# Values of recurrence and attention made as tokens by features in seven of eight mixing heads

## What is computed

```python
u = rms_norm(h, ln_mix_pre[l])
hq, hf, hi, hg, aq, ak, av = jnp.split(u @ w_in[l], split_at, axis=-1)
o_rec = hgrn2_mixer(hq, hf, hi, hg, lb_all[l], hgrn_norm[l])
o_att = dilated_attention_mixer(aq, ak, av)
mixed = jnp.concatenate([o_rec, o_att], axis=-1) @ w_out[l]
```

## Time and profile before

| | |
|---|---|
| median of 3 runs | 1771.32 us (1771.08 to 1771.66) |
| profiled execution, its own time | 1771.09 us |
| its span, first to last instruction | 1769.3 us |
| TensorE matmul busy | 1755.0 us, 99% of the span |
| DVE, ACT, POOL busy | 1254.6, 942.8 and 612.6 us |
| mean granted clock of TensorE | 0.998 |

### The profile page before, as it was taken

One profiled execution on the slowest core, in us unless ns is written; L12 is line 12 of the kernel. 1 busy time (PEld: TensorE's weight loads), 2 busy tenths in 40 slices (PEclk: granted clock), 3 DMA queues, 4 the chain that ended last, 5 costly groups with the idle time before them and its releaser, 6 DMA issues.

```text
span 1769.3 us, 29586 instructions
## 1 busy us (share of the span) xinstructions
PE 1755.0 (99%) x10201; PEld 1543.0 (87%) x10201; DVE 1254.6 (71%) x1594; ACT 942.8 (53%) x1254; POOL 612.6 (35%) x621
## 2 busy tenths in 40 slices
PE   9999999999999999999999999999999999999997
PEld 7888888888888888888888888888888888888886
DVE  6877777765598777777777644444987788887754
ACT  5544554554476555555555533334655567775532
POOL 1743345556603333111111322221262255550032
PEclk9999999999999999999999999999999999999999
DMA  8444444436565555555555555556455444444453
GB/s 314 176 177 167 165 167 167 167 143 247 184 237 189 189 190 190 190 190 190 190 190 190 169 190 186 194 185 220 168 190 202 167 167 167 167 167 163 169 188 119
DMA packets 51152, 326.61 MB, mean 185 GB/s; under 512 B 5792, under 2 KB 6432, under 8 KB 18464
## 3 DMA queue, kind: packets, MB, share of 16 engines
q1 hardware_dynamic: 49952, 323.86, 50.9%
q10 hardware_dynamic: 1152, 2.11, 0.4%
HBM read 323.85 MB, written 2.10 MB: 184 GB/s over the span
## 4 chain that ended last, share of the span: by engine, by line
PE 97%; DVE 1%; ACT 1%; DMA 0%; issue 0%; ACTq 0%; DVEq 0%
PE ps L1844 59%; PE ps L1845 30%; PE ps_lev L1844 1%; PE ps_sc L1883 1%; PE ps_lev L1919 1%; PE ps_lev L1969 1%; PE ps_t L1873 1%; PE ps_lev L1845 1%; DMA x_in<-in_x_turned 0%; PE bank_b L1974 0%; DVE wlo L993 0%; PE bank_a L1888 0%; DVE o_out L1702 0%; PE bank_a L1894 0%; PE ps_t L2190 0%; ACT whi L480 0%
## 5 line engine op out<-in xcount | busy, mean ns | idle before, releaser
L1844 PE MATMUL ps<-act_a,whi 128*128 128x512 f32 x3056 | 1069.4, 394 | 0.0
L993 DVE TENSOR_TENSOR wlo<-stage,whi 128x2048 fp32r<-128x2048 f32 (+1 forms) x314 | 689.0, 2195 | 245.8 <-ACT whi L480 240.9
L1845 PE MATMUL ps<-act_a,wlo 128*128 128x256 f32 x3056 | 854.3, 280 | 0.0
L1844 PEld LDWEIGHTS ps<-act_a,whi 128*128 128x128 f32 x3056 | 573.8, 188 | 125.6 <-issue 1.0
L480 ACT ACTIVATE whi<-stage 128x2048 fp32r<-128x2048 f32 (+1 forms) x314 | 565.9, 1802 | 122.6 <-DMA stage<-in_w_down 105.0
L1845 PEld LDWEIGHTS ps<-act_a,wlo 128*128 128x128 f32 x3056 | 574.0, 188 | 0.4
L1844 PE MATMUL ps<-big,whi 128*128 128x512 f32 x1536 | 534.4, 392 | 0.0
L1845 PE MATMUL ps<-big,wlo 128*128 128x256 f32 x1536 | 429.3, 280 | 0.0
L487 ACT ACTIVATE small<-ps 128x256 f32<-128x256 f32 x240 | 91.9, 383 | 533.3 <-PE ps L1845 533.2
L1844 PEld LDWEIGHTS ps<-big,whi 128*128 128x128 f32 x1536 | 288.4, 188 | 63.4
L1845 PEld LDWEIGHTS ps<-big,wlo 128*128 128x128 f32 x1536 | 288.4, 188 | 0.1
(11 more groups left out here) (378 smaller groups left out, 1354.5 us busy)
## 6 DMA issues: line engine op xcount, KB each, us to landing
stage<-in_w_a SPq DMA_DIRECT2D x166, 1024.0 KB, 4.8
stage<-in_w_b SPq DMA_DIRECT2D x86, 1024.0 KB, 4.8
stage<-in_w_down SPq DMA_DIRECT2D x64, 704.0 KB, 4.0
stage<-in_w_a SPq DMA_DIRECT2D x8, 256.0 KB, 8.7
mem_raw<-in_memT SPq DMA_DIRECT2D x1, 2048.0 KB, 9.3
mem_again<-in_memT SPq DMA_DIRECT2D x1, 2048.0 KB, 9.1
x_in<-in_x_turned ACTq DMA_DIRECT2D x7, 256.0 KB, 9.4
x_in<-in_xT SPq DMA_DIRECT2D x3, 512.0 KB, 5.8
```

The source lines that it names most:

```text
L993: dve.tensor_tensor(wlo[:, slot, part], stage[:, slot, part], whi[:, slot, part].bitcast(F32), ALU.subtract).then_inc(w_lo, 1)
L1844: pe.matmul(dst, whi[:, slot, c * P:(c + 1) * P], act, start=start, stop=False)
L1845: return pe.matmul(dst[:, T:2 * T], wlo[:, slot, c * P:(c + 1) * P], act[:, 0:T], start=False, stop=stop)
```

## The change

In heads 1 to 7 the blocks hi and av are used together. The 128 tokens of a tile are the stationary side, cut from `x_hi` or `x_lo`, and 256 columns move: 128 output features of hi and 128 of av, out of two weight slots side by side. `tile_values` does that for token tiles 0 and 1. The result is tokens by features at once, the sum of all three products in one half bank, so one DVE instruction (`values_scaled`) with the token's norm as a scalar per partition writes both values; the transposes, the two `turned` copies, two `evac`, two `add` and two `scaled` fall away. `norm_by_token`, once in head 1, turns the norm into two columns. The order of blocks in a head becomes hf, hq, aq, ak, then hi and av, then hg. Both slots of the pair are given free together, behind the second token tile. Head 0 stays. The positions of `hi` and `lo` for the later blocks move too.

```diff
-            def evac(u, b, ahead=0, bank=None):
+            def evac(u, b, ahead=0, bank=None, units=1):
 
 
                 act.wait_ge(w_used, u + ahead + 1)
                 act.wait_ge(out_free, u + 1)
-                act.activation(small[:, b, :], (ps[:, b, :] if bank is None else bank)[:, T:2 * T], ACT.Copy).then_inc(small_ready, 1)
+                act.activation(small[:, b, :], (ps[:, b, :] if bank is None else bank)[:, T:2 * T], ACT.Copy).then_inc(small_ready, units)
...
@@ -630,25 +626,20 @@
                 hi(start, i, 8, 5)
                 evac(u + 3, 1 - behind)
                 hi(start, i, 8, 6)
-                evac(u + 4, behind)
                 hi(start, i, 8, 7)
                 attention_out(before)
-                turned(vtok, "i_turned", "vtok_ready", i)
-                evac(u + 5, 1 - behind)
-                hi(start, i, 8, 8)
                 inverse_root(var[:, :], (s("var_ready"), before + 1), s("o_norm"))
                 if not memory:
                     cross(i)
                 attention_exp(i)
                 recurrence_out(before)
-                evac(u + 6, behind)
+                hi(start, i, 8, 8)
+                evac(u + 6, behind, units=3)
                 if memory:
                     hi(start, i, 8, 9)
                 tanh(eg, hgx, "hg_lin", "hg_tanh", i)
                 if memory:
                     cross(i)
-                turned(avtok, "av_turned", "avtok_ready", i)
-                if memory:
                     evac(u + 7, 1 - behind)
                     hi(start, i, 8, 10)
                 if behind:
@@ -1022,6 +1013,25 @@
                     dve.scalar_tensor_tensor(out=dst, in0=tmp[:, b, half], scalar=SCALE, in1=rstd[:, half],
                                              op0=ALU.mult, op1=ALU.mult).then_inc(s("aq_ready"), 1)
 
+            def norm_by_token():
+
+                dve.wait_ge(s("i_turned"), 1)
+                tiles = iT[:, :].rearrange("p (c t) -> p c t", c=2)
+                link(dve.tensor_tensor(tiles, rstd[:, :].rearrange("p (c t) -> p c t", c=2),
+                                       ident[:, :].unsqueeze(1).to_broadcast([P, 2, P]), ALU.mult))
+                link(dve.tensor_reduce(by_token, tiles, AX_X, ALU.add))
+
+            def values_scaled(i, u, b, t):
+
+                if t == 0:
+                    wait(dve, "tile_values", i)
+                    wait(dve, "hg_out", i)
+                    wait(dve, "att_out", i)
+                else:
+                    dve.wait_ge(w_used, u + 1)
+                dve.tensor_scalar(values[:, :, t, :], ps[:, b, 0:T].rearrange("p (v d) -> p v d", v=2),
+                                  by_token[:, t:t + 1], None, ALU.mult).then_inc(out_free, 1)
+
             def twice_gated(e, x, tanh_done, n):
 
                 dve.wait_ge(s(tanh_done), n)
...
@@ -1256,32 +1265,29 @@
                 query_made(i)
                 add(u + 2, behind)
                 lo(start, i, 8, 5)
-                scaled(u + 2, behind, iT[:, :], "i_ready")
+                queries_scaled(u + 2, behind)
                 add(u + 3, 1 - behind)
                 lo(start, i, 8, 6)
-                queries_scaled(u + 3, 1 - behind)
-                add(u + 4, behind)
+                scaled(u + 3, 1 - behind, akT[:, :], "ak_ready")
+                values_scaled(i, u + 4, behind, 0)
+                recurrence_variance(before)
                 lo(start, i, 8, 7)
-                scaled(u + 4, behind, akT[:, :], "ak_ready")
-                recurrence_variance(before)
                 place_levels(i, range(4))
                 attention_split(before)
-                add(u + 5, 1 - behind)
-                lo(start, i, 8, 8)
-                scaled(u + 5, 1 - behind, avT[:, :], "av_ready")
+                values_scaled(i, u + 5, 1 - behind, 1)
                 if not memory:
                     place_levels(i, range(4, LEVELS))
                 attention_max(i)
                 recurrence_normed(before)
+                lo(start, i, 8, 8)
                 add(u + 6, behind)
-                if memory:
-                    lo(start, i, 8, 9)
                 scaled(u + 6, behind, hgx[:, :], "hg_lin", factor=0.5)
                 recurrence_split(before)
                 if memory:
                     place_levels(i, range(4, LEVELS))
                 attention_weights(i)
                 if memory:
+                    lo(start, i, 8, 9)
                     add(u + 7, 1 - behind, dst=mkv[:, bass.ds(i, 1), :].squeeze(1))
                     lo(start, i, 8, 10)
                 gate_made(i)
@@ -1862,6 +1868,20 @@
                 await_block(start, i, per, j, u)
                 cells((start + j) % NS, bank, xs, order, ready=ready).then_inc(w_used, 1)
 
+            def tile_values(start, i, u, b, slots, t):
+
+                if t == 0:
+                    pe.wait_ge(w_lo, i * 8 + (start + 6))
+                pe.wait_ge(out_free, u + 1)
+                dst = ps[:, b, 0:T].rearrange("p (v d) -> p v d", v=2)
+                for c in range(KT):
+                    cell, tile = slice(c * P, (c + 1) * P), slice(t * P, (t + 1) * P)
+                    x_hi, x_lo = act_a[:, c, 0:T][:, tile], act_a[:, c, T:2 * T][:, tile]
+                    pe.matmul(dst, x_hi, whi[:, slots, cell], start=c == 0, stop=False)
+                    pe.matmul(dst, x_hi, wlo[:, slots, cell], start=False, stop=False)
+                    ins = pe.matmul(dst, x_lo, whi[:, slots, cell], start=False, stop=c == KT - 1)
+                ins.then_inc(*((w_used, 2) if t else (s("tile_values"), 1)))
+
             def column_sums(dst, srcs, waits, done):
 
                 for n, src in enumerate(srcs):
...
@@ -2014,23 +2033,23 @@
                 whole(start, i, 8, 1, u + 1, 1 - behind, act_a)
                 whole(start, i, 8, 2, u + 2, behind, act_a)
                 whole(start, i, 8, 3, u + 3, 1 - behind, act_a)
-                whole(start, i, 8, 4, u + 4, behind, act_a)
+                pair = slice((start + 4) % NS, (start + 4) % NS + 2)
+                tile_values(start, i, u + 4, behind, pair, 0)
                 attention_out(before)
                 recurrence_summed(before)
-                value_turned(i)
                 early_levels(i)
-                whole(start, i, 8, 5, u + 5, 1 - behind, act_a)
+                tile_values(start, i, u + 5, 1 - behind, pair, 1)
                 attention_scores(i)
                 if memory:
                     whole(start, i, 8, 6, u + 6, behind, act_a)
                     levels(i, range(4, LEVELS + 1))
                 else:
                     last_block(start, i, u, behind)
-                attention_value_turned(i)
                 if memory:
                     pe.wait_ge(s("xs_mem"), KT)
                     whole(start, i, 8, 7, u + 7, 1 - behind, xs_mem)
                 if behind:
+                    pe.wait_ge(out_free, u + 8)
                     recurrence_weighted(i)
 
             first_head()
```

49 lines of the change are left out of this document (23 added, 26 removed).

## The result

The changed kernel took 1778.04 us, the median of six runs (1777.93 to 1779.44), the kernel before 1771.30 (six runs, 1771.08 to 1771.66). The ratio is 1.0040, with a 95% interval from 1.0027 to 1.0053: 0.4% slower. The forecast was 1776.7 us in a range from 1773.0 to 1780.5.

A forecast was written before the change was run, and what follows sets the result against it. TensorE, busy 99%, was taken as the bound. Products +1.2, transposes -2.5, waits in heads 6 and 7 +3.3 and +3.6 gave +5.6 us on 1771.1: 1776.7 us, range 1773.0 to 1780.5.

The forecast's parts named there:

- The end of heads 6 and 7: `hi` and `lo` put the chain 3.75 us back; TensorE waits 3.3 us in head 6, 3.6 in head 7.
- a rival at 0.04: Clock falls to 1.2 GHz in two new waits, costing 1.7 us each: 1780 us; chance 0.04.
- The products of the pair: Heads 1 to 7: 224 groups of three matmuls, each 0.0055 us dearer than a cell: +1.2 us.
- the two pieces: Rival: the pair's moving side in two pieces of 128 columns costs up to +7.4 us: 1784; chance 0.06.
- the prediction's rival: Weight loads become the bound in the pair, 0.57 us a group: +50 us, 1826 with the waits; chance 0.01.
- The transposes: Those of hi and av fall away in seven heads, 0.36 us each: -2.5 us, bounds -1.9 to -3.2.
- Block `start + 5`: Wanted a block earlier by the pair's first token tile; in time by 0.7 us, costed at nothing.
- none of `start + 8`: Its load starts a block later, some 8 us in the loop's heads; about 4 us remain, so no wait.
- head 1 has no wait at `attention_turned`: `add` comes 1.9 us later, `attention_weights` ends at 105.5, TensorE asks at 105.6: nothing, by a tenth.
- The cover in heads 2 to 5: The memory block behind hg gives 5.5 us more before TensorE asks, so the later `hi` and `lo` cost nothing.

The follow-up runs named there:

- experiment 7: Changed kernel with hi and av packed by halves, first slot freed earlier, `hi` and `lo` near former places, head 1's `lo` back behind the levels: 1770.45 us.
- experiment 2: Changed kernel plus small matmuls with unused results, filling TensorE's pauses before `attention_turned` and before the cell waiting for `mix_done` of head 6: 1777.67 us.
- experiment 12: The changed kernel run and profiled once more, nothing altered: 1780.00 us, five runs.
- experiment 5: Changed kernel with the pair's 256 moving columns as one contiguous piece of one slot, values wrong: 1781.41 us.
- experiment 10: Kernel before, with only `hi` and `lo` of block `start + 8` in heads 6 and 7 moved to the change's places: 1781.45 us.
- experiment 4: Changed kernel with the change in heads 1 to 5 alone, heads 6 and 7 in the order of before: 1771.17 us.
- experiments 6 and 7: Changed kernel, hi and av packed by halves, first slot freed earlier: 1772.23 us; the same with head 1's `lo` back behind the levels: 1770.45 us.
- experiment 11: Kernel before, with `hi` and `lo` of block `start + 8` moved to the change's places in head 6 only: 1775.88 us.
- experiment 9: Packed-by-halves kernel with four forms of the three-product group by head, weights stationary in heads 2 to 5, values wrong: 1769.22 us, one run.
- experiment 3: Changed kernel with `hi` and `lo` of block `start + 8` in heads 6 and 7 back at their places before the change: 1779.96 us.

## Why the prediction was right, and where its sizes were off

**Bound and side.** That the change is worth what it does to TensorE's own stream plus the waits that it opens held; so did the side and, in the first six runs, the range. The five later runs gave a median of 1780.0, just inside it, with two of the five above it.

**The end of heads 6 and 7: mechanism and size as forecast.** I take experiment 7 as the measure, the same products without these waits (44.23 and 44.61 us between the marks). Head 6: a wait of 3.3 us forecast, 47.50 - 44.23 = 3.3 measured (the row's idle time, 3.11, counts from the modelled end of the product before). Head 7: 3.6 us forecast; where no clock fell, in experiment 2, 48.43 - 44.61 = 3.8, and the same 3.8 in experiment 12, since the mark comes when DVE's chain is done. Of its two waits the first was forecast at 394.5 - 392.4 = 2.1 and is 2.11; the second was left 1.5. Its idle time is 1.22 where the cells between the two ran at the full clock (experiment 5), and 0.35 to 0.93 where some of them ran at the lower one and took up part of it. Experiment 10 shows that the two places alone make these waits, experiment 4 that the whole loss comes from heads 6 and 7, and experiments 6 and 7 that the waits go once the slot comes free earlier and the two pieces of work stand near their places of before.

**The clock: a rival at 0.04 that took place.** Its size was right (3.4 us at the lower level, 1.7 each, as it put it; experiment 11 gives 1.6), its chance far too low. The rows at the end of the kernel showed a single pause, and from it I took two falls in the new, shorter ones for unlikely. Here it fell with ten of twelve pauses of 1.9 to 3.2 us: sometimes within them (2.7 us into that of head 6 in the changed kernel's first profile), sometimes up to 1.5 us after their end (experiment 5). It fell with all five of about 2 us, and with two of the seven of about 3 us it did not. The Trainium skill (TensorE: Matmul & The Clock Gate, Why this matters for your kernels) warns against idle gaps between bursts of matmuls. The ten falls bear the warning out, but the page has longer gaps in mind than the five of about 2 us, and here the clock fell with those too. The forecast put this term at nothing: it is 49.79 - 48.43 = 1.4 us up to the mark in head 7 and 0.5 behind it, 1.9 in the first profile. In the median it is smaller than that: the median of experiment 2, without a fall, is only 0.4 us below the changed kernel's.

**The products of the pair: mis-sized.** The step "each 0.3525 - 0.347 = 0.0055 us dearer: +1.2 us" took the nearest row, but in that row the weights stand still. With x stationary a group costs 0.360: 224 x 0.013 = +2.9 us. It is no matter of the two pieces (experiment 5) nor of the stage (experiment 9), but of what stands still. Weight loads did not become the bound: a group with three loads of 0.19 us takes 0.36, not 0.57, with their busy share at 87% before and after. The Trainium skill (Perfetto Trace Analysis, Identifying the Most-Contended Engine) judges TensorE's room by that share together with the matmul work done per time. Read by the share alone, as in the prediction's rival, it does not fit this trace.

**The transposes.** -2.5 us with a lower bound of -3.2. A head of the loop is only 0.02 us shorter, and its 32 groups cost 0.42 more; so the transposes were worth 0.44 a head by this estimate, -3.1 in all. Pair and transposes cancel: between the marks experiment 7 is 0.1 us below the kernel before, where the forecast had 1.3.

**Costed at nothing, and right.** Block `start + 5` came in time in every head, no product of the pair and none of `start + 8` waits, head 1 has no wait at `attention_turned` (`add` of hg there was put at about 102.5 and came at 102.30). The cover in heads 2 to 5 held. What I had not seen is that the late slots bind the two pieces of work of heads 6 and 7 to their late place (experiment 3).

**Sum.** Forecast: +1.2 - 2.5 + 3.3 + 3.6 = +5.6. In the first profile from mark to mark: -0.1 (pair and transposes) + 3.3 + 3.8 (waits) + 1.9 (clock) = +8.9, and so has the table. By the medians of the first six runs, where most were 1.4 us shorter than the profiled one, the distance to the forecast's +5.6 is 1.1. That it is so small is in part luck. The groups came 1.7 us dearer than put, and the clock cost something that the sum had left out; against these, the transposes were worth 0.6 us more, and in the profiles the part ahead of head 1, which the change does not touch, ran 0.6 us shorter.

## What to carry to other kernels

Work that is off the critical path in a loop's body may be on it in the last copies of that body, where the block that covered it is missing: follow a moved pair of conversions through each copy. A slot given free later takes away places where its next load's conversions could stand, even if that load is in time. And where TensorE is busy for 99%, allow for more than a new pause's length: here the clock fell with ten of twelve pauses of 1.9 to 3.2 us, and one of 2.9 us cost 4.6.

## What the hardware showed beside that

- Ahead of the end of the kernel, a stretch at 1.2 GHz lasted 3.4 us (seven times) or 6.8 (three times) in these profiles, about pauses of 1.9 to 3.2 us. It came neither with each such pause nor with the same one in two executions of one kernel.
- At 1.2 GHz a cell takes 0.64 us, less than twice its 0.347 at 2.4.
- 256 moving columns cost 0.1175 us with weights stationary and 0.120 with x stationary, 512 and 256 together 0.347 and 0.352. In both forms that is 0.0025 us more for each matmul whose stationary tile comes from x. The tiles have the same size; why they differ is open.
